# Retention queries and gates of a hybrid mixer: pairs of weight tiles by seven half-tile products in one stretch, kept in device memory, with the output tiles one head later

## Chip, cores, metric

The kernel runs on one core of one Trainium2 chip. The metric is the device time of one execution in microseconds, the median over runs. TensorE (PE) does the matmuls, ACT and DVE read its results from PSUM, POOL works on SBUF beside them, and SP issues most of the DMAs.

## What is computed

The reference runs two blocks one after the other on 512 tokens (528 with the 16 meta tokens in the second block) of width 1024, all in float32. The first block mixes gated DeltaNet heads with differential attention. The second is FFN1, a hybrid mixer and FFN2. The change is in the mixer:

```python
def hybrid_mixer(u, pos, k_top, w_in, w_ret_out, w_att_out, w_mix_out):
    proj = u @ w_in
    rq, rk, rv, rg, aq, ak, av, iq, ik, iw, g_ret, g_att = jnp.split(proj, offs, axis=-1)
    rq = rope(rq.reshape(B, T, RET_HEADS, RET_DK), pos)
    rk = rope(rk.reshape(B, T, RET_HEADS, RET_DK), pos) * (RET_DK ** -0.5)
    rv = rv.reshape(B, T, RET_HEADS, RET_DV)
    yr = retention(rq, rk, rv)           # chunked, with decays; then an rms norm over RET_DV
    yr = (jax.nn.silu(rg) * yr) @ w_ret_out
    ...
    ya = dsa_attention(aq, ak, av, iq, ik, iw, k_top).reshape(B, T, ATT_W) @ w_att_out
    merged = jax.nn.sigmoid(g_ret) * yr + jax.nn.sigmoid(g_att) * ya
    return merged @ w_mix_out
```

There are 4 retention heads. A head has 256 query and 256 key channels (two weight tiles of 128 columns each) and 512 value and 512 gate channels (four tiles each). `w_ret_out` brings each head's 512 channels to 8 output tiles.

## The kernel before

Activations lie in SBUF as channels by tokens. A float32 matmul is made of three in the `fp32r` type: each operand is split into a rounded high part and a low part, and `mm3` (L2504, which calls L2502) adds hi·hi, lo·hi and hi·lo. Weights come in blocks of 128 × 1024 (512 KB), in the order of use, through a ring of 4 tiles (`w_raw`). SP issues the loads; ACT makes the rounded part `w_hi` (`w_split` and `ahead`, L985), POOL the rest `w_lo` in four pieces of 128 × 256 (`low`, L3049). ACT, DVE and POOL each run a fixed program in order.

`results()` (L57) lists every PE result in order with its number of weight blocks. From the list follow the block numbers and, by the loop around L475, the PSUM place of each result: 8 banks, mostly used as 4 slots of two banks in rotation. PE's `begin(key)` (L2496) waits until the former holder of the place has been read out ("evacuated"). `dense` (L2537) multiplies one tile of 128 weight columns with the 512 or 528 tokens: 8 × 3 matmuls. `wide` (L2857) makes the values of a head: tokens are the stationary operand, weights the moving one, four blocks. `total` sums the squares of a norm.

The FFNs already use jobs of seven products (Strassen-Winograd). A job multiplies two weight tiles by 512 tokens. With weights and tokens each cut in halves, `product` (L2771) makes seven products of half tiles, P1, P5, P6, P2, P7, P3, P4, each 12 matmuls on 256 tokens, 84 in all. ACT and DVE make sums and differences of weight quarters (S1 to S4, whose rounding is L1060 and low part L2046); POOL makes the low parts of plain quarters (`raw_low`, L3055) and sums of token halves once per FFN (`x_sums`, L3094 to L3099). The products are combined on the way out of PSUM.

Retention, per head `hd`, on PE (loop at L2989): the second query tile `rq` (the first came earlier), two key tiles `rk`, the values `rv` by `wide`, gate tile `rg` 0, five score tiles `rs`, gate 1, four tiles `ry` of scores and state with values, gate 2, the norm's sum `rn`, gate 3, the next head's first query tile (behind the last head, the first tile of the mixing gate `gr`), and the eight output tiles `wr`. Behind the last head come `gr` 1 to 7, then `mx` (the last projection) and FFN2. ACT's program for a head (L1529 to L1570) copies queries and keys out, rounds them after DVE's rotation (`rotate` in DVE's part; L2391 to L2397, low parts L2402), rounds values (L1547) and scores (L1555), and copies `ry` to `ret_y`:

```python
for d in range(4):
    copy_out(("ry", hd, d), ret_y[:, d, :])
copy_out(("rg", hd, 2), rg[2], ACT.Silu)
```

The attention output tiles `ao` 0 to 7 stand on PE just before retention; DVE evacuates the last ones into `ya_late` (L2379). `h`, the residual, and `ya`, the attention's result, stay in SBUF over the retention stage.

Of the kernel before, what the change touches and what calls it, by code (L numbers as in the profile page):

```python
# [56 lines left out]
def results():  # L57
# [86 lines left out]
    for j in range(KD):  # L144
        add(("ao", j), 1)
    for hd in range(RET_H):
        if hd:
            add(("rq", hd, 1), 1)
        for j in range(2):
            add(("rk", hd, j), 1)  # L150
        add(("rv", hd, 0))
        add(("rv", hd, 1))
        add(("rv", hd, 2), 4)

        add(("rg", hd, 0), 1)
        for kt in range(NQ + 1):
            add(("rs", hd, kt))
        add(("rg", hd, 1), 1)
        for d in range(4):
            add(("ry", hd, d))  # L160
        add(("rg", hd, 2), 1)
        add(("rn", hd))
        add(("rg", hd, 3), 1)
        add(("rq", hd + 1, 0) if hd + 1 < RET_H else ("gr", 0), 1)
        for j in range(KD):
            add(("wr", hd, j), j % 2)
    for j in range(1, KD):
        add(("gr", j), 1)
# [21 lines left out]
JOBS = ffn_jobs()  # L190
PRODUCTS = ["P1", "P5", "P6", "P2", "P7", "P3", "P4"]
# [23 lines left out]
def job_at(i, n):  # L215
    return (i - 1) * len(JOBS) + n

# [27 lines left out]

def ffn_results(add, i):
# [5 lines left out]
    add(("wx", i))  # L252
    add(("wy", i))
    for n in range(len(JOBS)):
        for bank in BANKS:
            add((bank, i, n), 2 if bank == "pa" else 0)
# [195 lines left out]
for _key, _ in RESULTS:  # L452
# [42 lines left out]
    elif _key[0] == "iq":  # L495
        _p = ([4, 0, 2, 3][_key[1]], 1)
    elif _key == ("iw_t",):
        _p = (5, 1)
    elif _key[0] == "lam":
        _p = (3, 1)  # L500
    elif _key[0] in ("PT", "PV"):
        _p = (2 + (_key[0] == "PV"), 1)
    else:
        _p = (2 * (_main % SLOTS), 2)
        _main += 1
# [8 lines left out]
for _key, _n in RESULTS:  # L514
# [7 lines left out]
    elif _key[0] in ("dv", "rv"):  # L522
# [9 lines left out]
FFN_FIRST = {i: BLOCK["pa", i, 0] for i in (1, 2)}  # L532
FFN_BLOCKS = 2 * len(JOBS)
assert FFN_BLOCKS % RING == 0


def ffn_of(b):

    return next((i for i, first in FFN_FIRST.items() if first <= b < first + FFN_BLOCKS), None)


def whole(b):

    return b - sum(FFN_BLOCKS for first in FFN_FIRST.values() if b >= first + FFN_BLOCKS)
# [8 lines left out]
def last_product(tile):  # L553

    return max(g for g in range(len(PRODUCTS) * len(JOBS)) if g % (2 * RING) // 2 == tile) + 1

# [89 lines left out]
def build(nc, w_dram, x_dram, meta_dram, const_dram, small_dram, rot_dram, dec_dram, out_dram):  # L646
    with ExitStack() as ctx:
# [9 lines left out]
        w_lo = [sb(f"w_lo{i}", [P, 1024], F32R) for i in range(RING)]  # L657
        h = sb("h", [P, KD, TT])
# [16 lines left out]
        with ExitStack() as scope:  # L675
            yr = sb("yr", [P, KD, T], F32, scope)
            y_hi = sb("y_hi", [P, 4, T], F32R, scope)
            y_lo = sb("y_lo", [P, 4, T], F32R, scope)
        sb("x_area", [P, 2, KD * TT])
# [48 lines left out]
        with ExitStack() as mix:  # L728
# [3 lines left out]
            with ExitStack() as scope:  # L732
                aq = [mb("aq0", [P, 2, T], F32, scope)]
                av = [mb("av0", [P, NQ, 2 * P], F32, scope)]
            ya_late = mb("ya_late", [P, 4, T])
# [27 lines left out]
            with ExitStack() as scope:  # L763
                ret_y = mb("ret_y", [P, 4, T], F32, scope)
# [4 lines left out]
            with ExitStack() as scope:  # L769
                rg_late = mb("rg_late", [P, 2, T], F32, scope)  # L770
            rst_hi = mb("ret_score_hi", [P, sum(RET_WIDTHS)], F32R)
            rg = [rg_early[:, 0, :], rg_early[:, 1, :], rg_late[:, 0, :], rg_late[:, 1, :]]
            rstm = mb("ret_score_last", [P, M])
            rt_rot = mb("rt_rot", [P, 2, TT])
# [106 lines left out]
        def weight_part(i, n, name):  # L881
# [4 lines left out]
            return w_raw[b % RING][:, (name[2] == "2") * 512:(name[2] == "2") * 512 + 512]  # L886

# [55 lines left out]
        def _(sp):  # L943
# [10 lines left out]
            for b in range(RING, BLOCKS):  # L954
# [8 lines left out]
                sp.dma_start(w_raw[j][:], w_dram[b // RING, j]).then_inc(s_raw[j], 16)  # L963
            for a, (c0, c1) in enumerate(LAST_COLS):
# [6 lines left out]
        def _(act):  # L971
# [3 lines left out]
            def w_split(upto):  # L975

                while made["w"] < min(upto + 1, made["stop"]):
# [3 lines left out]
                    if i is not None:  # L981
                        act.wait_ge(s_prod, len(PRODUCTS) * job_at(i, 0) + last_product((b - FFN_FIRST[i]) % RING))
# [88 lines left out]

            def x_copy(i, j, c0):
# [31 lines left out]
            def ffn(i, c0):  # L1104
# [26 lines left out]
                def copy_on(dst, src, name, n):  # L1131

                    act.wait_ge(s_prod, product_at(i, n, name))
                    nc.scalar.activation(dst, slot((src, i, n))[:, 0:half], ACT.Copy).then_inc(s_seed, 1)

                for n in range(len(JOBS)):
# [10 lines left out]
                    copy_on(slot(("pb", i, n))[:, 0:half], "pa", "P1", n)  # L1147
# [8 lines left out]
                    copy_on(spare[:, 0:half], "pe", "P5", n)  # L1156
# [6 lines left out]
                    copy_on(slot(("pc", i, n))[:, 0:half], "pb", "P6", n)  # L1163
# [7 lines left out]
                    copy_on(spare[:, HALF:HALF + half], "pc", "P7", n)  # L1171
# [6 lines left out]
                made["w"], made["stop"] = b1, FFN_FIRST[2] if i == 1 else BLOCKS  # L1178
# [309 lines left out]
            act.wait_ge(s_rsd, made["rs"])  # L1488
            assert made["rs"] % 2 == GATE_RS
# [28 lines left out]
            pack(T)  # L1518
            for j in range(KD):
                ahead(("ao", j))  # L1520
            def sigmoid(key, i):
                if i >= 2:
                    act.wait_ge(s_gate, i - 1)
                wait_result(act, key)
                A.sig(nc.scalar.activation(square[i % 2][:, 0:T], slot(key)[:, 0:T], ACT.Sigmoid), *evac_at(key))

            wait_evac(act, ("ao", KD - 1))
            act.dma_start(rt_rot[:], rot_dram[:, 4:6]).then_inc(s_rtt, 16)
# [1754 lines left out]
```

## Time and profile before

| | us |
|---|---|
| median of 3 runs | 1926.14 |
| lowest, highest | 1925.92, 1926.17 |
| profiled execution | 1926.5 |
| its span | 1924.2 |
| PE busy in it | 1905.3 |
| DVE, POOL, ACT busy | 1182.2, 1016.6, 988.1 |

The span goes from the first to the last instruction of the profiled execution; its own time lies 2.3 us above it. Times in the rows below are counted from the start of the span. The mean granted clock of PE is 0.998 of full speed.

### The profile page before, as it was taken

To read this page: it belongs to the slowest core of one execution; us is meant where nothing else is said; L and a number is where in the kernel's file an instruction comes from. 1 tells how busy PE (TensorE), PEld (TensorE's weight loads), DVE (VectorE), ACT (ScalarE), POOL (GpSimd) and SP (SyncE) were. 2 spreads that over 40 slices of the span, in tenths; PEclk is the share of its full clock that TensorE was granted. 3 is DMA by queue.
4 is the path that set the end of the run, shared out by engine and by line. 5 is a ranking of instruction groups with operands and counts; after the bars stand their busy time and mean duration, and the time that the engine had idled before them with its cause. 6 is when DMAs were issued, how large, how long until landed. Compare 5 with 4: busy or idle time off the path is not lost.

```text
span 1924.2 us, 31665 instructions
## 1 busy us (share of the span) xinstructions
PE 1905.3 (99%) x11974; PEld 1677.7 (87%) x11974; DVE 1182.2 (61%) x2140; ACT 988.1 (51%) x1746; POOL 1016.6 (53%) x1100
## 2 busy tenths in 40 slices
PE   9999999999999999999999999999999999999998
PEld 6788777899999998789998888888888789999996
DVE  7845776877777757985442353334334367777765
ACT  5634454667676656434443252333334357767663
POOL 6432212588487475553333444454444568858554
PEclk9999999999999999999999999999999999999999
DMA  5221111222333333222221312232222222323332
GB/s 198 88 66 45 45 34 34 75 90 89 112 108 102 107 121 107 73 96 67 67 66 52 119 55 94 77 98 83 83 77 77 88 99 80 118 89 121 104 106 88
DMA packets 49653, 168.36 MB, mean 87 GB/s; under 512 B 6368, under 2 KB 8544, under 8 KB 49504
## 3 DMA queue, kind: packets, MB, share of 16 engines
q1 hardware_dynamic: 46576, 160.85, 25.1%
q10 hardware_dynamic: 2928, 5.51, 0.8%
q8 instruction: 96, 1.57, 0.3%
q14 instruction: 53, 0.43, 0.1%
HBM read 164.24 MB, written 2.10 MB: 86 GB/s over the span
## 4 chain that ended last, share of the span: by engine, by line
PE 92%; DVE 6%; ACT 1%; issue 1%; DMA 0%; POOL 0%; DVEq 0%; ACTq 0%
PE slot L2502 90%; DVE qkv L1726 1%; DVE x_lo L2266 0%; PE slot L2971 0%; DVE xt L2258 0%; DVE x_lo L1972 0%; PE slot L2687 0%; DVE qkv L1723 0%; DVE xt L2005 0%; PE slot L2652 0%; DVE slot L1720 0%; DMA small<-small_in 0%; DVE square L2023 0%; DVE h L2000 0%; DVE xt L1679 0%
## 5 line engine op out<-in xcount | busy, mean ns | idle before, releaser
L3049 POOL TENSOR_TENSOR w_lo<-w_raw,w_hi 128x256 fp32r<-128x256 f32 x744 | 600.1, 841 | 717.0 <-ACT w_hi L985 709.5
L2502 PE MATMUL slot<-x_hi,w_hi 128*128 128x264 f32 (+2 forms) x1384 | 469.4, 339 | 1.1 <-DVE x_lo L2266 0.7
L2502 PE MATMUL slot<-x_hi,w_lo 128*128 128x264 f32 (+2 forms) x1384 | 456.8, 330 | 0.0
L2502 PE MATMUL slot<-x_lo,w_hi 128*128 128x264 f32 (+2 forms) x1384 | 455.9, 329 | 0.0
L3055 POOL TENSOR_TENSOR w_lo<-w_raw,w_hi 128x512 fp32r<-128x512 f32 x168 | 218.4, 1311 | 151.8 <-ACT w_hi L1060 149.4
L2502 PEld LDWEIGHTS slot<-x_hi,w_hi 128*128 128x128 f32 x1384 | 260.3, 188 | 34.2 <-issue 7.6
L2502 PEld LDWEIGHTS slot<-x_lo,w_hi 128*128 128x128 f32 x1384 | 260.2, 188 | 25.2
L2502 PEld LDWEIGHTS slot<-x_hi,w_lo 128*128 128x128 f32 x1384 | 260.5, 188 | 24.0 <-issue 1.4
L985 ACT ACTIVATE w_hi<-w_raw 128x1024 fp32r<-128x1024 f32 x189 | 197.3, 1052 | 142.9 <-PE slot L2502 135.5
L2046 DVE TENSOR_TENSOR w_lo<-slot,w_hi 128x512 fp32r<-128x512 f32 x224 | 154.0, 688 | 95.2 <-ACT w_hi L1060 88.8
L2502 PE MATMUL slot<-x_sums_hi,w_hi 128*128 128x264 f32 (+1 forms) x640 | 180.7, 282 | 1.2 <-issue 1.2
L2502 PE MATMUL slot<-x_sums_hi,w_lo 128*128 128x264 f32 (+1 forms) x640 | 180.8, 283 | 0.0
L2502 PE MATMUL slot<-x_sums_lo,w_hi 128*128 128x264 f32 (+1 forms) x640 | 180.6, 282 | 0.0
L1060 ACT ACTIVATE w_hi<-slot 128x512 fp32r<-128x512 f32 x224 | 133.1, 595 | 39.6 <-PE slot L2502 19.8
L1060 ACT ACTIVATE w_hi<-w_raw 128x512 fp32r<-128x512 f32 x168 | 105.8, 630 | 44.4 <-PE slot L2502 44.3
L2502 PE MATMUL slot<-f_parts_hi,w_lo 128*128 128x264 f32 (+1 forms) x448 | 126.8, 283 | 0.0
L2502 PE MATMUL slot<-f_parts_hi,w_hi 128*128 128x264 f32 (+1 forms) x448 | 126.6, 283 | 0.0
L2502 PE MATMUL slot<-f_parts_lo,w_hi 128*128 128x264 f32 (+1 forms) x448 | 126.6, 283 | 0.0
L2502 PEld LDWEIGHTS slot<-x_sums_hi,w_hi 128*128 128x128 f32 x640 | 120.4, 188 | 1.5 <-issue 1.5
L2502 PEld LDWEIGHTS slot<-x_sums_lo,w_hi 128*128 128x128 f32 x640 | 120.5, 188 | 0.0
L2502 PEld LDWEIGHTS slot<-x_sums_hi,w_lo 128*128 128x128 f32 x640 | 120.4, 188 | 0.0
L2502 PE MATMUL slot<-w_hi,x_hi 128*128 128x512 f32 (+1 forms) x288 | 102.1, 355 | 0.0
(411 smaller groups left out, 4194.4 us busy)
## 6 DMA issues: line engine op xcount, KB each, us to landing
w_raw<-weights SPq DMA_DIRECT2D x301, 512.0 KB, 3.2
h<-x_t ACTq DMA_DIRECT2D x4, 512.0 KB, 6.7
dec<-decays ACTq DMA_DIRECT2D x4, 264.0 KB, 3.1
const<-consts SPq DMA_DIRECT2D x1, 576.0 KB, 6.6
at_rot<-rotations ACTq DMA_DIRECT2D x1, 528.0 KB, 4.1
ix_rot<-rotations ACTq DMA_DIRECT2D x1, 528.0 KB, 5.7
rt_rot<-rotations ACTq DMA_DIRECT2D x1, 528.0 KB, 3.6
w_raw<-weights SPq DMA_DIRECT2D x2, 256.0 KB, 4.3
```

The costliest lines, as they stand in the source:

```text
L985: nc.scalar.activation(w_hi[b % RING][:], w_raw[b % RING][:], ACT.Copy).then_inc(s_hi, 1)
L1060: nc.scalar.activation(w_hi[j][:, cols], weight_part(i, n, name), ACT.Copy).then_inc(s_ohi, 1)
L1726: ins = nc.vector.scalar_tensor_tensor(qkv[:, j, i:T], ps[:, 0:T - i], cw(3 - i), qkv[:, j, i:T], ALU.mult, ALU.add)
L2046: V.sig(nc.vector.tensor_tensor(w_lo[j][:, cols], weight_part(i, n, name), w_hi[j][:, cols].bitcast(F32), ALU.subtract), s_slo, sum_at(i, ...
L2502: return nc.tensor.matmul(out, lhsT, rhs, start=start, stop=stop, skip_group_check=onto)
L3049: nc.gpsimd.tensor_tensor(w_lo[j][:, piece], w_raw[j][:, piece], w_hi[j][:, piece].bitcast(F32), ALU.subtract).then_inc(s_lo, pieces)
L3055: nc.gpsimd.tensor_tensor(w_lo[j][:, cols], weight_part(i, n, name), w_hi[j][:, cols].bitcast(F32), ALU.subtract).then_inc(s_rlo, 1)
```

## The change

The two query tiles of heads 1, 2 and 3 and the four gate tiles of each of the four heads become 11 jobs (`MIX_JOBS`), which PE makes in one stretch behind the keys and values of head 0, with the same `product` as in the FFNs. The token sums are `t2_raw` (made by POOL, four instructions for each of four pairs of channel tiles), their rounded parts `t2_hi` (ACT) and low parts `t2_lo` (DVE). Each job's two tiles are staged in SBUF (in `ret_y` among others) and SP stores them in device memory (`kept`). ACT's queue brings queries (`queries_in`) and gates (`gates_in`) back one head ahead of their use. `h` and `ya` go to device memory before the stretch and come back later; `rv_lo` and the scores' low part get buffers of their own.

A head on PE is now: values (head 0's come before the jobs) with the former head's `rn` behind the first value block, two output tiles of the former head, scores, the other six output tiles of the former head, the next head's keys, and `ry`. The last head ends with `gr` 0, `rn`, `gr` 1 and 2, its eight output tiles and `gr` 3 to 7. `rk` of head 0 gets other PSUM places; the slots of all later results are counted from the scores of head 0.

The core of the diff ("..." marks what is left out):

```diff
         add(("ao", j), 1)
+    for j in range(2):
+        add(("rk", 0, j), 1)
+    for i in range(3):
+        add(("rv", 0, i), 4 * (i == 2))
+    job_results(add, MIX)
     for hd in range(RET_H):
         if hd:
-            add(("rq", hd, 1), 1)
-        for j in range(2):
-            add(("rk", hd, j), 1)
-        add(("rv", hd, 0))
-        add(("rv", hd, 1))
-        add(("rv", hd, 2), 4)
-
-        add(("rg", hd, 0), 1)
+            for i in range(3):
+                add(("rv", hd, i), 4 * (i == 2))
+            for j in range(WR_EARLY):
+                add(("wr", hd - 1, j), j % 2)
         for kt in range(NQ + 1):
             add(("rs", hd, kt))
-        add(("rg", hd, 1), 1)
+        if hd:
+            for j in range(WR_EARLY, KD):
+                add(("wr", hd - 1, j), j % 2)
+        if hd + 1 < RET_H:
+            for j in range(2):
+                add(("rk", hd + 1, j), 1)
         for d in range(4):
             add(("ry", hd, d))
-        add(("rg", hd, 2), 1)
-        add(("rn", hd))
-        add(("rg", hd, 3), 1)
-        add(("rq", hd + 1, 0) if hd + 1 < RET_H else ("gr", 0), 1)
-        for j in range(KD):
-            add(("wr", hd, j), j % 2)
-    for j in range(1, KD):
+        if hd + 1 < RET_H:
+            add(("rn", hd))
+    add(("gr", 0), 1)
+    add(("rn", RET_H - 1))
+    for j in range(1, GR_EARLY):
+        add(("gr", j), 1)
+    for j in range(KD):
+        add(("wr", RET_H - 1, j), j % 2)
+    for j in range(GR_EARLY, KD):
         add(("gr", j), 1)
...
 JOBS = ffn_jobs()
+MIX = 3
+MIX_JOBS = [("rq", hd) for hd in range(1, RET_H)] + [("rg", hd, p) for hd in range(RET_H) for p in range(2)]
...
+    elif _key in (("rk", 0, 0), ("rk", 0, 1)):
+        _p = (6 * _key[2], 2)
+    elif _key[:2] == ("rv", 0):
+        _p = (2 * _key[2], 2)
+    elif _key[0] == "rn" and _key[1] + 1 < RET_H:
...
+                n, second = divmod(b - FFN_FIRST[MIX], 2)
+                n -= 3
+                if second and 0 <= n < len(MIX_JOBS):
+                    for bank in BANKS:
+                        wait_evac(sp, (bank, MIX, n))
+                    sp.dma_start(kept_dram[:, 2 * n:2 * n + 2, :], staged(n)).then_inc(s_kept[n % 2], 16)
...
+            for k in range(0, KD, 2):
+                act.dma_start(h_dram[:, k:k + 2, :], h[:, k:k + 2, TQ]).then_inc(s_hout, 16)
...
+            def att_out_away(j):
+
+                wait_evac(act, ("ao", j))
+                act.dma_start(ya_dram[:, j, :], ya[j]).then_inc(s_yaout, 16)
...
+            def mixer_jobs():
+
+                i, half, spare = MIX, T // 2, rs[(made["rs"] + 1) % 2]
+                keys_out(0, 0)
+                w_split(BLOCK["rk", 0, 0] + RING)
+                rotated_high(0, 0)
+                keys_out(0, 1)
+                w_split(FFN_FIRST[i] - 1)
+                turn(i, 0)
+                rotated_high(0, 1)
+                operand_high(i, 0, "A11")
+                operand_high(i, 0, "S1")
+                mix_sum_high(0)
+                operand_high(i, 0, "S2")
+                operand_high(i, 0, "A12")
+                for pair in range(1, KD // 2):
...
+                values_out(0)
+                operand_high(i, 0, "A22")
+                turn(i, 1)
...
+            act.dma_start(dec[:], dec_dram[:, 0]).then_inc(s_dec, 16)
+            act.wait_ge(s_yaout, 16 * KD)
+            mixer_jobs()
...
+                act.wait_ge(s_last, hd + 1)
+                A.sig(nc.scalar.activation(rvm_parts[32:32 + M, :], rvm[0:M, :], ACT.Copy), s_rvmhi, 2 * hd + 1)
+                A.sig(nc.scalar.activation(rvm_parts[0:M, :], rvm[0:M, :], ACT.Copy), s_rvmhi, 2 * hd + 2)
+                if hd + 1 < RET_H:
+                    act.dma_start(dec[:], dec_dram[:, hd + 1]).then_inc(s_dec, 16)
+                    queries_in(hd + 1)
+                    ahead(("rk", hd + 1, 0))
+                    keys_out(hd + 1, 0)
+                    ahead(("rk", hd + 1, 1))
+                    keys_out(hd + 1, 1)
+                    w_split(BLOCK["rk", hd + 1, 1] + RING)
+                    for a in range(2):
+                        rotated_high(hd + 1, a)
+                else:
+                    ahead(("gr", 0))
+                if hd == 0:
+                    for n in range(len(MIX_JOBS) - 2, len(MIX_JOBS)):
+                        wait_kept(act, n)
                 for d in range(4):
                     copy_out(("ry", hd, d), ret_y[:, d, :])
-                copy_out(("rg", hd, 2), rg[2], ACT.Silu)
...
+                if hd + 1 == RET_H:
+                    for k in range(0, KD, 2):
+                        act.dma_start(h[:, k:k + 2, TQ], h_dram[:, k:k + 2, :]).then_inc(s_hback, 16)
...
+            def rotate(hd, a):
+
+                name, w = (("rq", T), ("rk", TT))[a]
+                if name == "rq" and hd:
+                    dve.wait_ge(s_rql, 32 * hd)
+                else:
...
+                if hd:
+                    for j in range(WR_EARLY, KD):
+                        ret_out(hd - 1, j)
+                if hd + 1 < RET_H:
+                    rotate(hd + 1, 0)
+                    rotate(hd + 1, 1)
...
+            def wide(keys, aside=None):
 
                 sl = [begin(k) for k in keys]
                 b = BLOCK[keys[-1]]
                 for i in range(4):
+                    if aside and i == 1:
+                        aside()
...
+            keys_of(0)
+            wide([("rv", 0, i) for i in range(3)])
+            for n in range(len(MIX_JOBS)):
+                for name in PRODUCTS:
+                    product(MIX, n, name, T // 2, lambda k: mix_tokens(n, name, k))
             for hd in range(RET_H):
                 if hd:
-                    dense(("rq", hd, 1), SEQ, (x2_hi, x2_lo))
-                for j in range(2):
-                    dense(("rk", hd, j), ALL, (x2_hi, x2_lo))
-                wide([("rv", hd, i) for i in range(3)])
...
-                dense(("rg", hd, 1), SEQ, (x2_hi, x2_lo))
+                if hd:
+                    for j in range(WR_EARLY, KD):
+                        ret_out(hd - 1, j)
+                if hd + 1 < RET_H:
+                    keys_of(hd + 1)
...
                         raw_low(i, n + 1, "A22")
 
+            def mix_sums(pair):
+
+                b11, b12, b21, b22 = (t2_raw[:, pair, t, :] for t in range(4))
+                pool.wait_ge(s_t2raw, pair + 1)
+                G.own(nc.gpsimd.tensor_tensor(b22, b22, b12, ALU.subtract))
+                G.own(nc.gpsimd.tensor_tensor(b12, b12, b11, ALU.subtract))
+                G.sync()
+                G.own(nc.gpsimd.tensor_tensor(b11, b22, b11, ALU.add))
+                G.sync()
+                G.sig(nc.gpsimd.tensor_tensor(b21, b21, b11, ALU.subtract), s_t2sum, pair + 1)
+
+            def mixer_jobs():
+
+                for pair in range(KD // 2):
+                    mix_sums(pair)
+                for n in range(len(MIX_JOBS)):
+                    for name in RAWS:
+                        raw_low(MIX, n, name)
+
```

## Rows read from the trace of the kernel before

**Rows 1.** The page's busy times by engine: us, share, instructions.

```profile
PE 1905.3 (99%) x11974; PEld 1677.7 (87%) x11974; DVE 1182.2 (61%) x2140; ACT 988.1 (51%) x1746; POOL 1016.6 (53%) x1100
```

**Rows 2.** The chain that ended last, shares of the span by engine.

```profile
PE 92%; DVE 6%; ACT 1%; issue 1%; DMA 0%; POOL 0%; DVEq 0%; ACTq 0%
```

**Rows 3.** Timeline of PE, retention stage: start, us long, instruction.

```profile
1072.74 0.28 PE L2502 MATMUL slot<-x_hi,w_hi 128*128 128x264 f32 x1
...
1173.67 0.40 PE L2502 MATMUL slot<-x_hi,w_hi 128*128 128x512 f32 x1
...
1179.23 0.28 PE L2502 MATMUL slot<-x_hi,w_hi 128*128 128x264 f32 x1
...
1190.84 0.39 PE L2502 MATMUL slot<-w_hi,x_hi 128*128 128x512 f32 x1
...
1222.33 0.39 PE L2502 MATMUL slot<-rqk_hi 128*128 128x512 f32 x1
...
1226.36 0.48 PE L2502 MATMUL slot<-x_hi,w_hi 128*128 128x512 f32 x1
...
1232.00 0.39 PE L2502 MATMUL slot<-ret_score_hi,rv 128*128 128x512 f32 x1
...
1240.14 0.48 PE L2502 MATMUL slot<-x_hi,w_hi 128*128 128x512 f32 x1
```

**Rows 4.** Timeline of PE, FFN2; in brackets idle time before.

```profile
1605.67 0.28 PE L2502 MATMUL slot<-x_lo,w_hi 128*128 128x256 f32 x1
...
1606.60 0.36 PE L2502 MATMUL slot<-x_sums_hi,w_hi 128*128 128x256 f32 x1 [0.66 <-issue]
...
1829.33 0.28 PE L2502 MATMUL slot<-x_hi,w_hi 128*128 128x256 f32 x1
...
1839.26 0.28 PE L2502 MATMUL slot<-x_hi,w_hi 128*128 128x256 f32 x1
```

**Rows 5.** Windows of retention and FFN2's jobs: us, busy by engine, clock.

```profile
core 0: us, PE busy (x) PEld busy (x) DVE busy (x) ACT busy (x) POOL busy (x), PEclk, DMA share, GB/s
1110.00:1532.00 422.00, 422.00 (x2066) 349.58 (x2064) 173.44 (x248) 155.18 (x204) 203.50 (x260) 1.00 0.25 82
1610.00:1878.00 268.00, 268.00 (x2269) 268.00 (x2269) 197.22 (x372) 180.39 (x363) 184.74 (x155) 1.00 0.32 107
```

**Rows 6.** Timeline of ACT, around head 0's keys and values.

```profile
1191.04 0.61 ACT L1040 ACTIVATE square<-slot 128x528 f32<-128x528 f32 x1 [3.46 <-PE slot L2502]
1191.54 1.14 ACT L1543 ACTIVATE rqk_hi<-xt 128x512 fp32r<-128x512 f32 x2
1197.66 1.18 ACT L1543 ACTIVATE rqk_hi<-xt 128x528 fp32r<-128x528 f32 x2 [4.97 <-DVE xt L2397]
1198.74 1.99 ACT L985 ACTIVATE w_hi<-w_raw 128x1024 fp32r<-128x1024 f32 x2
...
1216.97 1.94 ACT L1547 ACTIVATE rv<-slot 128x1024 fp32r<-128x1024 f32 x2 [11.85 <-PE slot L2502]
...
1234.21 0.60 ACT L1040 ACTIVATE ret_y<-slot 128x512 f32<-128x512 f32 x1 [0.47 <-PE slot L2502]
```

**Rows 7.** Timeline of POOL: low pieces of blocks, sums before FFN2.

```profile
1181.06 4.38 POOL L3049 TENSOR_TENSOR w_lo<-w_raw,w_hi 128x256 fp32r<-128x256 f32 x4 [3.16 <-ACT w_hi L985]
...
1187.65 2.82 POOL L3049 TENSOR_TENSOR w_lo<-w_raw,w_hi 128x256 fp32r<-128x256 f32 x4 [2.22 <-ACT w_hi L985]
...
1588.51 0.75 POOL L3097 TENSOR_TENSOR x_sums<-x_sums 128x256 f32<-128x256 f32 x1
...
1591.29 1.72 POOL L3094 TENSOR_TENSOR x_sums<-x_sums 128x256 f32<-128x256 f32 x1
```

**Rows 8.** Timeline of DVE: ao7's evacuation, rotation of queries and keys.

```profile
1072.94 0.69 DVE L2379 TENSOR_TENSOR ya_late<-slot,rs 128x512 f32<-128x512 f32 x1 [4.80 <-PE slot L2502]
...
1181.33 1.22 DVE L2393 TENSOR_TENSOR square<-square,rt_rot 128x512 f32<-128x512 f32 x1
...
1192.27 1.29 DVE L2402 TENSOR_TENSOR rqk_lo<-xt,rqk_hi 128x512 fp32r<-128x512 f32 x2 [6.29 <-ACT rqk_hi L1543]
...
1196.92 0.70 DVE L2397 TENSOR_TENSOR xt<-xt,square 128x528 f32<-128x528 f32 x1
```

**Rows 9.** DMA issues: count, KB each, us from issue to landing.

```profile
dec<-decays ACTq DMA_DIRECT2D x4, 264.0 KB, 3.1
...
out<-h SPq DMA_DIRECT2D x2, 256.0 KB, 2.2
```

**Rows 10.** Waits of PE from 1072 to 1605: total, count, longest.

```profile
PE slot L2502 <- ACT square L1525: 0.7, 1, 0.7
```

More of the change, by code:

```diff
@@ L243, in before_job, with job_results @@
     return JOBS[n - 1][1] if JOBS[n - 1][0] == kind else None
+def job_results(add, i):
+    add(("wx", i))
+    add(("wy", i))
+    for n in range(len(JOBS_OF[i])):
+        for bank in BANKS:
+            add((bank, i, n), 2 if bank == "pa" else 0)
 def ffn_results(add, i):
@@ L251, in ffn_results @@
         add(("up", i, f), 1)
[L252 to L256, printed above, removed]
+    job_results(add, i)
     for d in range(KD):
@@ L1584, in _ @@
+            for j in range(KD):
+                ahead(("wr", RET_H - 1, j))
+            for j in range(GR_EARLY, KD):
+                ahead(("gr", j))
+                if j == GR_EARLY:
+                    x_high(2, 0, M, merged_hi)
+                sigmoid(j)
                 x_high(1, j - 1, M, merged_hi)
@@ L2751, in _, with product @@
                 out_part(j, 0, KD)
+            part_of = {"P1": 0, "P2": 1, "P3": 2, "P5": 3, "P6": 4, "P7": 5, "P4": 6}
+            token_part = {"P1": (0, 0), "P2": (1, 0), "P3": (1, 1)}
+            token_sum = {"P5": "T1", "P6": "T2", "P7": "T3", "P4": "T4"}
+            f_name = {"P1": "B11", "P2": "B2", "P3": "B2"}
+            bank_of = {"P1": "pa", "P2": "pa", "P5": "pe", "P6": "pb", "P3": "pb", "P7": "pc", "P4": "pc"}
+            seeded = {"P6": "P1", "P7": "P6", "P4": "P7"}
+            def product(i, n, name, half, source):
+                operand = OPERANDS[PRODUCTS.index(name)]
+                j, cols = operand_place(i, n, operand)
+                key, opens = (bank_of[name], i, n), name in ("P1", "P5")
+                if opens:
+                    begin(key)
+                if operand in SUMS:
+                    pe.wait_ge(s_slo, sum_at(i, n, operand))
+                else:
+                    pe.wait_ge(s_rlo, raw_low_at(i, n, operand))
+                if name in seeded:
+                    pe.wait_ge(s_seed, seed_at(i, n, seeded[name]))
+                for k in range(KD // 2):
+                    x = source(k)
+                    w = [a[j][:, cols.start + k * P:cols.start + k * P + P] for a in (w_hi, w_lo)]
+                    m = mm3(slot(key)[:, 0:half], w, x, opens and k == 0, k == KD // 2 - 1, not opens)
+                m.then_inc(s_prod, 1)
             def ffn(i, parts):
@@ L3225, in stream @@
                 w.reshape(4, P, KD, P)[:, :, j:j + 2].transpose(1, 2, 0, 3).reshape(P, 1024)))
-    for j in range(1, KD):
+    keys_of(0)
+    wide(part("rv", 0, 512))
+    for job in MIX_JOBS:
+        at = job[1] * 256 if job[0] == "rq" else job[1] * 512 + job[2] * 256
+        for j in range(2):
+            turned(part(job[0], at + j * P, P))
+    for hd in range(RET_H):
+        if hd:
+            wide(part("rv", hd * 512, 512))
+            ret_out(hd - 1)
+        if hd + 1 < RET_H:
+            keys_of(hd + 1)
+    for j in range(GR_EARLY):
+        cols(part("gr", j * P, P))
+    ret_out(RET_H - 1)
+    for j in range(GR_EARLY, KD):
         cols(part("gr", j * P, P))
```

556 lines of the change are left out of this document (341 added, 215 removed).

## Prediction

> **What bounds the kernel now.** I read the busy times first. TensorE (PE) works for 1905.3 of 1924.2 us [rows 1], and the chain that ended last runs through it for 92% [rows 2]. So the time follows what PE is given to do and the few places where it stands still; an engine elsewhere matters only where PE waits for its last step. The profiled execution took 1926.5 us, 2.3 us outside its span, and the median of the runs is 1926.14, 0.36 less: I sum against 1926.5 and take 0.4 off at the end. About 0.2% (3.9 us) is what a measurement of this kernel can tell from no change.
>
> Second, PE's own timeline, where starts of successive results give the price of a piece of work, waits included. In the retention stage [rows 3] a 128-column weight tile against 512 tokens lasts 1173.67 → 1179.23 = 5.56 us. In FFN2 [rows 4], whose jobs have the form the change uses, a pair of tiles by seven products lasts 1829.33 → 1839.26 = 9.93 us. The granted clock is 1.00 over both stretches [rows 5], so both are prices at the 2.4 GHz level. A pair of tiles is 2 × 5.56 = 11.12 as it is now; seven half products for eight would be 9.73 of that by columns alone. Third, the helpers' timelines around one retention head [rows 6 to 8], because they decide whether PE can go on.
>
> **Removed and added on PE.** The three queries of heads 1 to 3 are two tiles each, the gates four tiles for each of four heads: 6 + 16 = 22 tiles × 5.56 = 122.3 us. In their place stand 11 jobs × 9.93 = 109.2 us. The net is −13.1. Scores, values, keys, retention products and output tiles are moved and not changed in number. I take FFN2's 9.93 for the new jobs: there DVE and ACT had the up-projection's combining and its activation beside the same operand work; here only copies to the staging tiles.
>
> **Bank of the first key tile.** rk(0,0) now takes the banks of the last attention output tile, ao7. That tile's successor on PE begins at 1072.74 today [rows 3], and DVE's reading of ao7 ends at 1072.94 + 0.69 = 1073.63 [rows 8]: PE waits 0.9 us, between 0.9 and 1.0. **+0.9**
>
> **Start of the jobs.** POOL makes sixteen token sums of 128×256. In front of FFN2 one takes 0.75 us, or 1.72 where DVE reads SBUF beside it [rows 7]: 12 us or 27.5 us for all sixteen. They stand in POOL's program behind the low parts of the value blocks, while PE works on values for 1222.33 − 1190.84 − 5.56 = 25.9 us [rows 3], and the lows are done a block ahead, so some 15 to 20 us are left. Behind the last sum come roundings on ACT, a value copy of about 1.0 (one of the pair at 1216.97 [rows 6]) and lows on DVE of about 1.3 (the pair at 1192.27 [rows 8]) before the first product gets its bank. FFN2's own start shows what it costs when it is nearly in time: of the 0.93 from 1605.67 to 1606.60, 0.66 is idle [rows 4], say 0.7. I take 2.0: nearer the hidden end, plus half the value copy's and the low's chain. Bounds 0.7 and 3.5. **+2.0**
>
> **End of the jobs.** The first weight block behind them, that of rk(1,0), can only be rounded when the last product has freed its tile: 0.2 + 1.05 on ACT and the four pieces on POOL, 2.82 to 4.38 [rows 7], so 4.1 to 5.7. Scores cover 1226.36 − 1222.33 = 4.03 [rows 3]. I take 0.4 of 0.1 to 1.7. **+0.4**
>
> **A new order on ACT, and who waits for it.** This is the term that decides. In each of heads 0 to 2 the next head's keys now come right before the four products ry on PE, and the next head's values right behind. The value tiles take the banks of ry0, ry1 and ry2; those are free when ACT has copied them out, and in ACT's program the four copies stand behind the rounding of the next head's rotated queries and keys. That rounding cannot begin before the keys exist. Today's chain gives its length [rows 6]: from the last key matmul 0.2 to the key copy, 0.50 from the copy to the next instruction (1191.04 → 1191.54), 0.95 for one weight rounding put ahead (half of 1.99 with its gap), 1197.66 − 1191.54 = 6.12 from the first query rounding over DVE's lows and the key's rotation to the first key rounding, and 1.08 for the two of that (1197.66 → 1198.74): 8.85 us. Then the three copies, 2 × 0.5 + 0.60 [rows 6]: 10.5. PE has the ry products as cover, 1240.14 − 1232.00 = 8.14 [rows 3]. It waits 2.4 us if that chain runs as undisturbed as it does today at this place.
>
> It will not quite: today POOL is idle or between blocks while the keys are rotated at 0.70 us an instruction, and 1.22 where POOL's low pieces of a weight block run at the same time; those pieces then take 4.38 for four and not 2.82 [rows 7, 8]. In the new order the block rounded ahead puts POOL's four pieces into this chain. About three DVE instructions meet them: 3 × 0.52 = 1.5 more, stall 3.9. This is the value for heads 1 and 2. The next head's queries come back from device memory, their load issued behind the score roundings; in heads 1 and 2 six output tiles (33 us) cover that, in head 0 nothing stands between but the keys: a 264 KB load lands 3.1 us after issue, a 256 KB store in 2.2 [rows 9]. The rotation of these queries begins later by some of that; I take 4.6 there. 3.9 + 3.9 + 4.6 = **+12.4**. Bounds: 3 × 2.4 = 7.2 plus a little for head 0, 7.4; and 4.5 × 2 + 4.4 ≈ 13.4 with a fourth DVE instruction met. Queued behind the late copies on ACT are the gates' silu and the norm's root, whose readers (DVE's gate products, then the output tiles) come after a value stage of 25.9 us: nothing is late there. What ACT rounds next is the second value block, which the pieces put ahead cover.
>
> The Trainium skill, page "SBUF — State Buffer", section "Who interferes with whom", has it that a DVE instruction with two SBUF inputs and a GpSimd instruction that reads SBUF exclude each other, the second fully waiting. By that each DVE instruction would wait for a whole piece of about 0.7, the three together +2.2 in place of +1.5, the sum below 4.7 and the time near 1930.8. The row's 1.22 against 0.70 bears out the contention at 0.52, less than a whole piece; I go by the row.
>
> **Costs taken at nothing.** The norm's total behind the first value block has about 0.7 us to spare by the same chain: 0, up to 1. The stores of the job results and the trips of h and ya to memory run on queues that are nearly idle, a store of 256 KB landing in 2.2 us and none waited for within less than a job of 9.93 [rows 4, 9]; uncovered, one costs its 2.2. Output tiles run one head later, same count. The stage behind retention starts with the 0.7 us wait on ACT's sigmoids that it has today [rows 10]. A gain or loss in these beyond 1 us I exclude.
>
> **Sum.** −13.1 + 0.9 + 2.0 + 0.4 + 12.4 = +2.6: own time 1929.1, median 1928.7. With the low ends, −13.1 + 0.9 + 0.7 + 0.1 + 7.4 = −4.0, 1922; with the high ends, −13.1 + 1.0 + 3.5 + 1.7 + 13.4 + 1.0 = +7.5, 1933.
>
> **The rivals.**
> *Faster.* The chain before ry's copies doesn't hold PE: the key copy, the roundings and DVE's rotation overlap ry so that little is left. For it: DVE has less to do than PE at this place, and query rotation is prepared earlier. Against it: 8.85 us on the timeline, undisturbed, is already longer than ry's cover. Sum −13.1 + 0.9 + 1.0 + 0.2 = −11.0: 1915.
> *Slower.* POOL's token sums meet DVE through most of the value stage, at 1.72 each [rows 7]: 27.5 us against 15 to 20. The jobs begin 5 to 12 us late, and since a late start also finds the weights' lows behind the sums, nothing is given back. It decides when more than about half of the sixteen meet DVE (8 × 1.72 + 8 × 0.75 = 19.8). For it: FFN2's rows show three in a row at over 1.2; against it: five or more at 0.74 in the same place, and DVE's own work in the value stage is small. About +5 to +8: 1934.
> *No gain from seven products.* The jobs take as long as two tiles, 11.1, since their low parts and sums fall behind PE. Net 0 in place of −13.1: 1941.8. Against it, FFN2's 9.93 with more work beside it.
>
> **Chances.** The forecast 0.68, of it 0.07 below 1922.3 and 0.12 above 1930.0; the faster rival 0.13; the slower 0.15; no gain from the products 0.04. Faster by over 0.2%: 0.07 + 0.13 = 0.20. Slower by over 0.2%: 0.12 + 0.15 + 0.04 = 0.31. Within: 0.49. The forecast's own range is 1922 to 1932; the one for 8 in 10 reaches part way into both neighbours, 1918 to 1934.
>
> **What would show it.** Each job 9.9 us from its first matmul to the next job's; the start of the first job 2 us behind the last value matmul; in each head 0 to 2 a gap on PE before the first value matmul, 3.9 to 4.6 us, named as a wait for ACT's copy to the retention output, and ACT's copies behind the key roundings; POOL's sixteen sums over before the value stage ends. A gap of under 1 us at the values makes the forecast wrong towards 1915; a gap of over 5 at the first job, or jobs over 10.3, makes it wrong upwards.

## The result and the profile after

The changed kernel takes 1940.3 us, median of 4 runs from 1937.89 to 1941.94; the kernel before takes 1926.09. The ratio is 1.0073, 95% interval 1.0055 to 1.009: slower by 14 us where no measurable change was forecast (1928.7, range 1918 to 1934). The profiled execution took 1941.94 us, span 1940.1 against 1924.2, so 15.9 us are to be found.

Busy times and the chain that ended last come first:

```profile
PE 1901.6 (98%) x12370; PEld 1694.7 (87%) x12370; DVE 1269.1 (65%) x2280; ACT 1030.3 (53%) x1846; POOL 1008.2 (52%) x1061
...
PE 86%; DVE 7%; ACT 2%; POOL 2%; issue 1%; DMA 1%; ACTq 0%; DVEq 0%
```

PE is busy 3.7 us less than in [rows 1], not the 13 that the products save, and holds 86% of the chain and not 92% [rows 2]. So PE both waits more and works slower. The waits of PE, from the last attention outputs to FFN2's start (total, times, longest; L1108 is the line of `copy_out`, L2592 makes the values' low part, L3339 the low pieces of weight blocks):

```profile
PE slot L2758 <- ACT ret_y L1108: 14.7, 3, 7.2
PE slot L2758 <- DVE rv_lo L2592: 3.1, 1, 3.1
PE slot L2758 <- DVE ya_late L2552: 0.8, 1, 0.8
PE slot L2758 <- ACT square L1108: 0.7, 1, 0.7
PE slot L2758 <- issue: 0.7, 1, 0.7
PE slot L2758 <- POOL w_lo L3339: 0.4, 2, 0.2
```

ACT's 0.7 of [rows 10] and the 0.7 of "issue" in front of FFN2 [rows 4] were there before, and so was one of POOL's two 0.2, which stands at 1052 us, ahead of the stage. The new ones stand on PE's timeline where they were forecast: at head 0's first key tile, at the first job, and at the values of heads 1, 2 and 3.

```profile
1075.01 0.39 PE L2758 MATMUL slot<-x_hi,w_hi 128*128 128x264 f32 x1 [0.78 <-DVE ya_late L2552]
...
1115.93 0.58 PE L2758 MATMUL slot<-x_hi,w_hi 128*128 128x256 f32 x1 [3.13 <-DVE rv_lo L2592]
...
1128.60 0.28 PE L2758 MATMUL slot<-x_hi,w_hi 128*128 128x256 f32 x1
...
1227.49 0.40 PE L2758 MATMUL slot<-rqk_hi 128*128 128x512 f32 x1
...
1259.17 0.76 PE L2758 MATMUL slot<-w_hi,x_hi 128*128 128x512 f32 x1 [7.22 <-ACT ret_y L1108]
...
1338.60 0.77 PE L2758 MATMUL slot<-w_hi,x_hi 128*128 128x512 f32 x1 [3.74 <-ACT ret_y L1108]
...
1417.61 0.47 PE L2758 MATMUL slot<-w_hi,x_hi 128*128 128x512 f32 x1 [3.74 <-ACT ret_y L1108]
```

From the second job's first matmul to the scores stand ten jobs: (1227.49 − 1128.60) / 10 = 9.89 us each, where [rows 4] gave 9.93. The products do what they are meant to. What is new is how long single matmuls last behind a wait. Windows of the gaps and of the stretches right behind them (us, busy time by engine with counts, granted clock, DMA):

```profile
core 0: us, PE busy (x) PEld busy (x) DVE busy (x) ACT busy (x) POOL busy (x), PEclk, DMA share, GB/s
1112.50:1115.80 3.30, 0.30 (x2) 0.00 (x0) 3.30 (x5) 3.28 (x6) 2.17 (x1) 0.89 0.12 14
1116.30:1121.80 5.50, 5.50 (x27) 5.50 (x27) 3.88 (x6) 2.18 (x6) 2.52 (x2) 0.50 0.49 176
1122.00:1128.00 6.00, 6.00 (x53) 6.00 (x52) 3.86 (x7) 3.32 (x8) 1.29 (x1) 1.00 0.24 78
1251.80:1259.10 7.30, 0.15 (x2) 0.06 (x1) 6.19 (x11) 2.82 (x6) 0.00 (x0) 0.72 0.05 22
1259.70:1265.20 5.50, 5.50 (x14) 3.97 (x13) 5.06 (x8) 4.29 (x4) 0.00 (x0) 0.50 0.00 0
...
1339.10:1343.80 4.70, 4.70 (x12) 3.50 (x11) 4.25 (x8) 4.32 (x4) 0.00 (x0) 0.50 0.00 0
...
1418.80:1422.20 3.40, 3.40 (x9) 2.30 (x9) 3.02 (x6) 3.37 (x4) 0.00 (x0) 0.51 0.00 0
1422.60:1428.00 5.40, 5.40 (x24) 3.90 (x23) 3.19 (x6) 1.12 (x2) 0.00 (x0) 1.00 0.01 3
```

Behind each of the four long gaps PE runs at 0.50, its 1.2 GHz level, for 3 to 6 us, and returns to 1.00; in [rows 5] the stage was at 1.00 throughout. A 256-column matmul then takes 0.213 us and not 0.118, one of 512 columns 0.427 and not 0.23. Summed over the slow matmuls that is 2.6 + 2.7 + 2.3 + 1.6 = 9.2 us.

The account in us of the span, each wait with its own length: products 11 × 9.89 − 22 × 5.56 = −13.5; first key tile +0.8; first job +3.1; values +14.7; half clock +9.2; POOL's low parts +0.2; sum +14.5. Another 1.3 lie ahead of everything changed: the last matmul in front of the first key tile starts at 1073.83 in this profile, at 1072.5 before and in the experiments' profiles of the changed kernel. They arise at 25.35 us, where PE waits 1.06 us for DVE in this execution and not in that of before. Together 15.8, where 15.9 were to be found. The four runs differ by 4 us and their mean clock with them, from 0.994 at 1937.89 us to 0.991 at 1941.94; the four of before lie within 0.25 us.

### The profile page after: what moved, and what is told of

It is laid out like the page before. It is cut to its first block, busy times and chain, and to the rows that moved or that the text cites. A ratio compares the mean times of both kernels' runs of the same rounds, so it can differ in the third digit from the quotient of the medians.

```text
span 1940.1 us, 32909 instructions
## 1 busy us (share of the span) xinstructions
PE 1901.6 (98%) x12370; PEld 1694.7 (87%) x12370; DVE 1269.1 (65%) x2280; ACT 1030.3 (53%) x1846; POOL 1008.2 (52%) x1061
## 4 chain that ended last, share of the span: by engine, by line
PE 86%; DVE 7%; ACT 2%; POOL 2%; issue 1%; DMA 1%; ACTq 0%; DVEq 0%
PE slot L2758 85%; DVE qkv L1899 1%; POOL w_lo L3339 1%; ACT w_hi L1053 1%; DVE x_lo L2439 0%; PE slot L3236 0%; DVE xt L2431 0%; DVE x_lo L2145 0%; DMA h<-x_t 0%; DMA square<-kept 0%; PE slot L2943 0%; DVE qkv L1896 0%; DVE xt L2178 0%; DVE dqk L1843 0%; DMA w_raw<-weights 0%
## 5 line engine op out<-in xcount | busy, mean ns | idle before, releaser
L3339 POOL TENSOR_TENSOR w_lo<-w_raw,w_hi 128x256 fp32r<-128x256 f32 x656 | 533.6, 847 | 676.7 <-ACT w_hi L1053 669.0
L2758 PE MATMUL slot<-x_hi,w_hi 128*128 128x264 f32 (+2 forms) x1340 | 436.4, 326 | 5.2 <-DVE rv_lo L2592 3.1
L2758 PE MATMUL slot<-x_hi,w_lo 128*128 128x264 f32 (+2 forms) x1340 | 424.9, 317 | 0.0
L2758 PE MATMUL slot<-x_lo,w_hi 128*128 128x264 f32 (+2 forms) x1340 | 424.3, 317 | 0.0
L3345 POOL TENSOR_TENSOR w_lo<-w_raw,w_hi 128x512 fp32r<-128x512 f32 x201 | 261.6, 1310 | 215.9 <-ACT w_hi L1128 212.5
L2758 PEld LDWEIGHTS slot<-x_hi,w_hi 128*128 128x128 f32 x1340 | 252.6, 188 | 30.6 <-issue 7.2
L2210 DVE TENSOR_TENSOR w_lo<-slot,w_hi 128x512 fp32r<-128x512 f32 x268 | 184.3, 689 | 112.2 <-ACT w_hi L1128 102.9
L1053 ACT ACTIVATE w_hi<-w_raw 128x1024 fp32r<-128x1024 f32 x167 | 174.0, 1052 | 106.0 <-PE slot L2758 103.2
L1128 ACT ACTIVATE w_hi<-slot 128x512 fp32r<-128x512 f32 x268 | 159.2, 595 | 50.5 <-DVE slot L2204 26.0
L1128 ACT ACTIVATE w_hi<-w_raw 128x512 fp32r<-128x512 f32 x201 | 126.6, 630 | 52.0 <-PE slot L2758 51.9
L2758 PE MATMUL slot<-w_hi,x_hi 128*128 128x512 f32 (+1 forms) x288 | 106.0, 368 | 14.7 <-ACT ret_y L1108 14.7
```

The source lines that it names most:

```text
L1053: nc.scalar.activation(w_hi[b % RING][:], w_raw[b % RING][:], ACT.Copy).then_inc(s_hi, 1)
L1128: nc.scalar.activation(w_hi[j][:, cols], weight_part(i, n, name), ACT.Copy).then_inc(s_ohi, 1)
L2210: V.sig(nc.vector.tensor_tensor(w_lo[j][:, cols], weight_part(i, n, name), w_hi[j][:, cols].bitcast(F32), ALU.subtract), s_slo, sum_at(i, ...
L2758: return nc.tensor.matmul(out, lhsT, rhs, start=start, stop=stop, skip_group_check=onto)
L3339: nc.gpsimd.tensor_tensor(w_lo[j][:, piece], w_raw[j][:, piece], w_hi[j][:, piece].bitcast(F32), ALU.subtract).then_inc(s_lo, pieces)
L3345: nc.gpsimd.tensor_tensor(w_lo[j][:, cols], weight_part(i, n, name), w_hi[j][:, cols].bitcast(F32), ALU.subtract).then_inc(s_rlo, 1)
```

## Experiments

All times are medians, beside the kernel before on the same chip (1926.0 to 1926.3); intervals are at 95%. Two theories stood at first: that the loss is waits and, as much again, an idle PE's half clock; or that a gap costs only its length and the slow matmuls have another cause.

**Gaps filled.** The waits stay, but PE works in them: matmuls whose result nobody reads.

```diff
+            def fill(bank, n):
+                for _ in range(n):
+                    mm(psum[bank // 2][:, bank % 2 * 512:bank % 2 * 512 + 512], x2_hi[:, 0, 0:P], x2_hi[:, 0, 0:512], True, True)
...
+            fill(5, 15)
             for n in range(len(MIX_JOBS)):
...
+                    fill(PLACE["ry", hd - 1, 3][0] + 1, [34, 17, 17][hd - 1])
                     wide([("rv", hd, i) for i in range(3)], lambda: total(("rn", hd - 1), 8, T))
```

> The changed kernel with matmuls of 512 columns that nobody reads put where TensorE stood still: 34 ahead of head 1's values (7.2 us of waiting), 17 ahead of those of heads 2 and 3 (3.8 us each), 15 ahead of the first job (3.3 us). The waits for ACT and DVE stay as long as they are. Theory: an idle TensorE is granted half its clock for some us afterwards, and 9.2 us of the loss is that; with the gaps filled the clock stays at 1.00 and the kernel takes 1940.3 - 9.2 = about 1931, with runs close together. Rival: the slow matmuls behind the gaps have another cause (the operands, contention for SBUF); then they stay slow and the time stays at 1940 or rises by what the filling overshoots.

1932.16 us, ratio 1.003 (1.0019 to 1.0041): 8.1 below the changed kernel, with 83 matmuls more. The windows behind the former gaps:

```profile
1114.60:1120.00 5.40, 5.40 (x47) 5.36 (x46) 4.45 (x7) 3.52 (x8) 2.55 (x2) 1.00 0.56 189
...
1255.50:1261.00 5.50, 5.18 (x23) 3.81 (x22) 4.98 (x8) 5.45 (x6) 0.00 (x0) 1.00 0.01 3
```

The same work on DVE, ACT and POOL beside it, and the clock is 1.00. It was the idling, not the operands or contention. The runs lie within 0.9 us.

**Gaps made in the kernel before.** PE is held ahead of each head's values by a chain of tiny ACT instructions.

```diff
+                for _ in range([2, 5, 9, 22][hd]):
+                    A.own(nc.scalar.activation(idle[:], rt_rot[:, 0, 0:8], ACT.Copy))
+                    A.sync()
+                act.sem_inc(s_idle, 1)
...
+                pe.wait_ge(s_idle, hd + 1)
                 wide([("rv", hd, i) for i in range(3)])
```

> The kernel before with TensorE held ahead of the values of each head by a chain of 2, 5, 9 and 22 tiny ACT instructions behind the copy of the last key tile: idle gaps of about 1.2, 2.2, 3.3 and 7 us. Nothing else is changed. Theory: a gap costs its own length and, from about the third on, 2 to 3 us more at half clock: 13.7 + 5 = 1945 in all. Rival: a gap costs only its length, 1940.

1942.46 us, ratio 1.0083 (1.0068 to 1.0098). Against the trace of before, the matmuls behind the four holds come 1.3, 2.1, 3.05 and 6.2 us later, together 12.6. Windows behind the third and in and behind the fourth gap:

```profile
1304.80:1310.00 5.20, 5.20 (x23) 4.05 (x24) 4.35 (x7) 1.10 (x2) 0.00 (x0) 1.00 0.00 0
1411.40:1417.30 5.90, 0.11 (x1) 0.00 (x0) 0.00 (x0) 5.08 (x23) 0.00 (x0) 0.88 0.24 89
1418.00:1422.60 4.60, 4.60 (x12) 3.49 (x11) 4.30 (x7) 0.56 (x2) 0.00 (x0) 0.50 0.01 2
```

Only the longest was followed by half clock, worth 2.3 us, though I had put the 3 us gap among those too. 12.6 + 2.3 and 1.0 at the kernel's start, at the same matmul as the 1.3 above, make the 16. With the jobs absent the same price appears.

**ACT's order.** The copies of `ry` 0 to 2 go ahead of the key roundings, and the norm's sum one value block later.

```diff
-                    for a in range(2):
-                        rotated_high(hd + 1, a)
+                    rotated_high(hd + 1, 0)
...
                 for d in range(4):
+                    if d == 3 and hd + 1 < RET_H:
+                        rotated_high(hd + 1, 1)
                     copy_out(("ry", hd, d), ret_y[:, d, :])
...
-                    if aside and i == 1:
+                    if aside and i == 2:
```

> The changed kernel with ACT copying the retention outputs 0 to 2 ahead of the rounding of the next head's keys, and the norm's sum behind the second value block in place of the first. Theory: the value tiles waited for these copies alone, so all three waits go (14.7 us) and with them the three slow stretches (6.6 us): 1940.3 - 21.3 = about 1919, which is below the kernel before. Rival: something else holds the values as well (the weight block's low part on POOL, or the norm's sum, which DVE has ready some 16.5 us behind the last key against 21 us for the second block): a wait of 1 to 3 us per head stays, and the time is 1924 to 1930.

1919.24 us, ratio 0.9965 (0.9951 to 0.998): faster than the kernel before. What is left of the waits:

```profile
PE slot L2759 <- DVE rv_lo L2593: 3.4, 1, 3.4
PE slot L2759 <- ACT ret_y L1108: 1.1, 1, 1.1
PE slot L2759 <- DVE ya_late L2553: 0.8, 1, 0.8
```

ACT's order made the three long waits (the next run leaves the sum in its place, and only 2.0 of them come back); 1.1 remain at head 1, where the queries come late.

**The norm's sum left where it was.** As above, with `i == 1`.

> The ACT order alone, with the norm's sum left behind the first value block. Theory: DVE has the squares some 16.5 us behind the last key matmul, and the first block ends 14.6 us behind it, so that a wait of about 2 us appears in heads 1 and 2 and of 4 to 5 in head 0, named after DVE's sum of squares; with a stretch of half clock behind the long one 1919.2 + 9 + 2 = about 1929. Rival: the squares are in time, and the place of the sum is worth nothing: 1919.

1935.73 us, ratio 1.0049 (1.0036 to 1.0063). The wait is there, and longer than worked out:

```profile
PE slot L2759 <- DVE square L2711: 10.0, 3, 3.8
PE slot L2759 <- DVE rv_lo L2593: 3.2, 1, 3.2
PE slot L2759 <- ACT ret_y L1108: 2.0, 1, 2.0
```

3 us and more in each head, not 2: DVE's lows and rotation meet POOL's pieces, 1.5 us that the 16.5 had left out. Of the 21 us that the order gives 16.5 are lost again; the changed kernel's long wait had hidden this second one.

**Queries earlier.** Head 1's are loaded right behind the jobs.

```diff
             mixer_jobs()
+            queries_in(1)
             gates_in(0)
...
-                    queries_in(hd + 1)
+                    if hd:
+                        queries_in(hd + 1)
```

> The changed kernel with the load of head 1's queries issued right behind the jobs, ahead of the gates, and no longer behind head 0's score roundings. Theory: the wait at head 1's values falls from 7.2 to the 3.8 of the other heads, the clock loss stays: 1940.3 - 3.4 = about 1937. Rival: head 0's wait is long for another reason (the last stores of the job outputs that are waited for ahead of its copies), and nothing changes.

1935.48 us, ratio 1.0045 (1.003 to 1.006). The wait at head 1 falls from 7.2 to 5.4 and not to 3.8. The queries are there, but DVE is not: it ends the scores' low parts at 1237.2 and then rotates beside POOL, which makes 24 low pieces in one run:

```profile
1237.30 1.04 DVE L2575 TENSOR_TENSOR xt<-square,rt_rot 128x512 f32<-128x512 f32 x1
...
1244.82 2.22 DVE L2586 TENSOR_TENSOR rqk_lo<-xt,rqk_hi 128x512 fp32r<-128x512 f32 x2 [0.77 <-ACT rqk_hi L1614]
```

ACT's copies follow right behind the key roundings, so the rival's stores hold nothing up. The rest of the 4.8 us is about what the half clock takes less in this profile than in the changed kernel's (6.0 us in the four stretches, not 9.2).

**Start of the jobs.** On top of ACT's order, the first half of head 0's values is rounded and its banks freed ahead of the last pair of token sums, and the seed of the third product is copied ahead of later weight roundings.

```diff
                 for pair in range(1, KD // 2):
+                    if pair == 3:
+                        values_out(0, (0,))
                     mix_sum_high(pair)
+                values_out(0, (1,))
                 operand_high(i, 0, "S3")
-                operand_high(i, 0, "S4")
-                values_out(0)
-                operand_high(i, 0, "A22")
-                turn(i, 1)
...
                     copy_on(slot(("pb", i, n))[:, 0:half], "pa", i, n, "P1")
+                    if n == 0:
+                        operand_high(i, 0, "S4")
+                        operand_high(i, 0, "A22")
+                        turn(i, 1)
+                        operand_high(i, n + 1, "A11")
```

DVE's program is changed alike.

> The kernel of the ACT order (copies of the retention outputs ahead of the key roundings), and the start of the jobs reordered: the first half of head 0's values is rounded, its low part made and its banks freed ahead of the last pair of token sums, and the copy that seeds the third product comes ahead of the later weight roundings. Theory: the first product waited for these banks behind everything else on DVE (3.4 us, and 1.6 us of half clock behind it); both go but for some 0.5 us in which the first weight's low part and the third product's seed are late: 1919.2 - 4.5 = about 1914.7. Rival: POOL's token sums set the start, as their last pair ends at the same time; then the wait stays above 2 us, now named after a low part of a sum or of a weight, and the time stays at 1918 or above.

1918.88 us, ratio 0.9961 (0.9947 to 0.9974), no clear difference from ACT's order alone. The wait at the first product is gone, and one of 2.3 stands ahead of the fifth, for which the trace names no engine:

```profile
PE slot L2768 <- issue: 2.9, 2, 2.3
PE slot L2768 <- ACT ret_y L1108: 1.6, 1, 1.6
```

Neither theory had that. The fifth product builds on a copy that ACT makes of the third one's result, and in ACT's program this stood behind a rounding for the next job that waits for DVE's sum.

**All of it.** The same with the early queries, and head 0's first key tile in banks 4 and 5:

```diff
-        _p = (6 * _key[2], 2)
+        _p = (4 + 2 * _key[2], 2)
```

> The reordered start and the ACT order, with head 1's queries loaded right behind the jobs, and the first key tile in another pair of banks than the last attention output tile. Theory: the 1.1 us wait at head 1's values and the 0.8 us wait for that output tile go too: 1914.7 - 1.9 = about 1912.8, all of the 13.1 us that the seven products save. Rival: the early load of 512 KB beside the gates' loads delays the weights, or the second key tile now waits for the first one's banks; 1914 to 1916.

1916.14 us, ratio 0.9944 (0.993 to 0.9957). The waits for `ry` and `ya_late` are gone from the list; the one ahead of the fifth product stays, with 1.6 us of half clock behind it, and is the 3 us that are missing.

**The first job's copies.**

```diff
                         turn(i, 1)
-                        operand_high(i, n + 1, "A11")
+                        copy_on(spare[:, 0:half], "pe", i, n, "P5")
+                        for taken in FREE["pc", i, n]:
+                            wait_evac(act, taken)
+                        copy_on(slot(("pc", i, n))[:, 0:half], "pb", i, n, "P6")
+                        for name in ("A11", "S1", "S2"):
+                            operand_high(i, n + 1, name)
```

> The kernel with all reorderings, and in the first job ACT copies the fifth and sixth product's... that is, the second and third product's results on ahead of the next job's weight roundings. Theory: the 2.1 us wait ahead of the first job's fifth product came from a copy that stood in ACT's program behind a sum which DVE had not made; it goes with its 1.6 us of half clock: 1916.1 - 3.7 = about 1912.4, which is the kernel before less the whole saving of the products (1926.1 - 13.1 = 1913.0). Rival: the low part of the first weight sum is what is late, the wait moves to the next product, 1915 to 1916.

1913.47 us (1913.26 to 1913.99), ratio 0.9933 (0.9919 to 0.9946), the best of all. The whole stage, with all 11 jobs, is at full clock:

```profile
1072.00:1530.00 458.00, 455.95 (x2715) 398.82 (x2714) 280.79 (x415) 211.67 (x323) 220.13 (x248) 1.00 0.38 122
```

12.9 us below the kernel before on the same chip, of the 13.1 to 13.5 that the seven products save. In the profile the span is 1911.9, 12.3 below, and the waits that the kernel before did not have add up to 1.3 (0.65 and 0.45 in front of products of the first job, 0.2 behind the jobs): 13.5 − 1.3 = 12.2. So no hidden cost of the products, of the trips to memory or of POOL's work shows.

## Why the prediction was wrong, point by point

**The step that failed** is the sum's rule that a stall costs its own length. "It waits 2.4 us", "stall 3.9", "I take 2.0": each entered the sum as it was. But PE went on at half clock behind each of the four long gaps in this profile, and that cost 9.2 us, most of the 11.6 by which the forecast is off. It was no term and no rival; the trace of before could not show it in this stage, since PE's longest wait there was 0.7 us [rows 10]. It shows the level once, at its own end, where PE has waited 1.77 us for DVE's squares and has 0.53 us of work left in the last 7.3:

```profile
1916.70:1924.00 7.30, 0.53 (x2) 0.00 (x0) 3.40 (x6) 0.89 (x2) 0.00 (x0) 0.50 0.71 246
```

The two runs that bear on it alone agree: filling the gaps gave 8.1 back, and a 6.2 us gap in the kernel before cost 2.3 more than itself. The Trainium skill, page "TensorE: Matmul & The Clock Gate", section "HAM oscillation — how this bites in real kernels", says that a TensorE that waits long enough falls back to half its clock and that the work behind each such wait then starts slow. The trace agrees, 0.50 in all four stretches; that rule should have been one of the rivals. Of the prediction's signs of being wrong one was met, and by this: the first job lasts 1128.60 − 1115.93 = 12.7 us, the others 9.9 on average.

**Products, −13.1.** Right: 9.89 a job, −13.5 in all.

**First key tile, +0.9.** Right: 0.8, and gone with another bank.

**Start of the jobs, +2.0.** Under-sized: 3.1, inside its bounds of 0.7 to 3.5. POOL:

```profile
1095.52 1.20 POOL L3422 TENSOR_TENSOR mix_sums<-mix_sums 128x256 f32<-128x256 f32 x1
...
1111.15 3.52 POOL L3345 TENSOR_TENSOR w_lo<-w_raw,w_hi 128x512 fp32r<-128x512 f32 x2
```

The sixteen sums took 1111.15 − 1095.52 = 15.6 us, between the 12 and 27.5 of [rows 7]; the slower rival, by which they set a delay of 5 to 12, did not come true. They end about 1.5 us before the values do. What was late was DVE's low part of the values, queued behind low parts of weights that were not yet needed, as was ACT's rounding ahead of it:

```profile
1113.46 1.28 DVE L2210 TENSOR_TENSOR w_lo<-slot,w_hi 128x512 fp32r<-128x512 f32 x2
1114.66 2.35 DVE L2592 TENSOR_TENSOR rv_lo<-slot,rv 128x1024 fp32r<-128x1024 f32 x2
```

**End of the jobs, +0.4.** Right: PE waits 0.2 for POOL there, at 1231.87.

**Waits at the values, +12.4.** Right in mechanism and nearly in size: 14.7. Heads 2 and 3's, forecast as 3.9 each, are 3.74. The chain before the first of them, on ACT and then POOL and DVE:

```profile
1326.68 0.61 ACT L1108 ACTIVATE ret_keys<-slot 128x528 f32<-128x528 f32 x1 [4.25 <-PE slot L2758]
...
1335.71 1.18 ACT L1614 ACTIVATE rqk_hi<-xt 128x528 fp32r<-128x528 f32 x2 [6.43 <-DVE xt L2579]
1336.79 2.04 ACT L1108 ACTIVATE ret_y<-slot 128x512 f32<-128x512 f32 x4
```

```profile
1328.32 4.19 POOL L3339 TENSOR_TENSOR w_lo<-w_raw,w_hi 128x256 fp32r<-128x256 f32 x4 [2.98 <-ACT w_hi L1053]
```

```profile
1328.86 1.88 DVE L2584 TENSOR_TENSOR rqk_lo<-xt,rqk_hi 128x512 fp32r<-128x512 f32 x2 [7.11 <-ACT rqk_hi L1614]
...
1331.83 1.24 DVE L2574 TENSOR_TENSOR xt<-ret_keys,rt_rot 128x528 f32<-128x528 f32 x1
```

The copies of `ry` begin 10.1 us behind the key copy, and DVE's instructions beside POOL's pieces are longer as foreseen: 1.88 for the pair of lows (1.29 in [rows 8]), 1.24 for 0.70. Together with a third the lengthening is 1.5 us. By the estimate from the Trainium skill, page "SBUF — State Buffer", section "Who interferes with whom", read as a full wait for each piece, it would have been 2.2; the trace shows less. Head 1's wait was mis-sized: 7.2 for 4.6. The queries' load had been counted with the 3.1 us of one alone [rows 9]; the chain shows 7.1 from issue to landing, while the decays' and the weights' loads were on the way too:

```profile
1236.78 7.10 DMA square<-kept
```

That load is worth 1.8 us of the wait, as the run with the queries earlier shows. What this wait has beyond the 3.74 of the other heads even then, 1.7 us, the sum did not have at all: DVE is free late there, and more than three of its instructions run beside POOL's pieces.

**Costs taken at nothing.** The norm's sum, "0, up to 1", was 0 in the changed kernel only because the values were late; with ACT's order put right it costs 10.0 us of waiting. That margin was worked out from the end of the stalled chain, not from the end of `ry`.

**Rivals.** The faster one needed the chain not to hold PE: false at this order, and true once the order was mended (1919.24 with ACT's order and the norm's sum moved, 1913.47 with the start of the jobs, the queries and the first key tile's banks mended as well, against its 1915). No gain from the products: false.

Why DVE is late at 25 us in this one profile, and in that of the gaps made in the kernel before, stays open; it is outside the change.

## What to carry to other kernels

Price a new wait on TensorE by its length and by the work behind it at half clock: here the changed kernel's four gaps of 3.5 to 7.4 us (by matmul starts) added 1.6 to 2.7 us each, while most of the shorter ones in all runs added nothing. Where an engine runs a fixed program, look for an instruction that frees PSUM banks and stands behind one that waits for another engine: moving three copies and one sum was worth 21 us, and each repaired wait uncovered the next, so list the next two before trusting a margin. When a saving does not show, compare the granted clock of stretches right behind the gaps before looking for contention.

## What the runs showed of the hardware that I had not expected

The clock does not follow the gap's length alone (all lengths here are by matmul starts). Behind 3.04 us of holding in the kernel before it stayed at 1.00; behind 3.52 in the changed kernel it fell to 0.50; and in the kernel with all of it but the first job's copies a gap of 2.40 us was followed, 1 us after work had resumed, by 3.4 us at half clock. The plainest pair is in one execution, that of the norm's sum left where it was: PE waits for that sum from 1339.03 to 1342.51 and from 1415.13 to 1418.62, 3.48 us both times, and goes on at 1.00 behind the first and at 0.50, again 1 us late, behind the second:

```profile
1339.30:1342.40 3.10, 0.12 (x1) 0.00 (x0) 2.83 (x6) 0.64 (x1) 0.00 (x0) 1.00 0.00 0
1342.60:1349.00 6.40, 6.40 (x27) 4.74 (x28) 5.84 (x10) 3.19 (x5) 0.00 (x0) 1.00 0.01 3
1415.30:1418.50 3.20, 0.23 (x1) 0.00 (x0) 2.92 (x6) 0.75 (x1) 0.00 (x0) 1.00 0.00 0
...
1419.70:1423.00 3.30, 3.30 (x10) 2.52 (x9) 2.82 (x5) 2.33 (x4) 0.00 (x0) 0.50 0.00 0
```

In the changed kernel itself two gaps of the same 3.96 us cost 2.3 and 1.6: behind the second the clock fell only 1.2 us after PE had gone on. So the price of a gap is a range and not one figure. That this is what spreads the runs is not shown: those of the changed kernel lie within 4 us, but those with the queries earlier, with four such gaps, within 1.1, and those of the kernel before within 0.25 in one series and 1.8 in another.
